# Recurrent mixer: sigmoids as tanh, roots and reciprocals as a power on GpSimd, and k and r loaded one tile ahead

## The reference, cut to what matters

```
w_log = -softplus(-(w0 + tanh(wd) @ w_up)) - 0.5
decay = exp(-exp(w_log))              # = exp(-const * sigmoid(w0 + ...))
a     = sigmoid(a0 + ad @ a_up)
kk    = head_l2norm(k * k_k)          # x * rsqrt(sum(x*x over the head) + 1e-12)
k_eff = k * (1 + (a - 1) * k_a)
...                                    # the recurrence over positions, y = its output
yn    = (y - mean) * rsqrt(var + 64e-5) * ln_g + ln_b     # per head
out   = (yn + bonus) * (sigmoid(gd) @ g_up)
```

## Time and profile before

| | |
|---|---|
| time, median of 3 | 4488.01 us (4481.62 to 4489.07) |
| profiled execution, its own time | 4496.26 us |
| its span | 4494.6 us |
| recurrent mixer phase in it | about 2068 to 2872 us |
| granted TensorE clock, mean | 0.961 of full speed |

### The profile page before, as it was taken

One profiled execution on the slowest core, in us unless ns is written; L12 is line 12 of the kernel. 1 busy time (PEld: TensorE's weight loads), 2 busy tenths in 40 slices (PEclk: granted clock), 3 DMA queues, 4 the chain that ended last, 5 costly groups with the idle time before them and its releaser, 6 DMA issues. The chain is left out here.

```text
span 4494.6 us, 74705 instructions
## 1 busy us (share of the span) xinstructions
PE 4000.6 (89%) x29550; PEld 2823.7 (63%) x29550; DVE 2819.5 (63%) x5982; ACT 1519.4 (34%) x3304; POOL 867.1 (19%) x908
## 2 busy tenths in 40 slices
PE   8989999988999899998989999898999788777776
PEld 6747887756888686786877778687444333333332
DVE  5674433775432566756666666335778888888885
ACT  3353242354433336613555554332111111111111
POOL 1101010100200101100000000000344444444443
PEclk9999999999999999998999999899999988999999
DMA  4213443301443310231000000333999999999998
GB/s 129 81 39 110 146 133 99 115 19 57 154 146 104 133 38 20 99 108 39 15 17 20 24 23 6 127 113 128 381 405 421 421 409 415 414 405 412 413 410 330
DMA packets 150605, 795.18 MB, mean 177 GB/s; under 512 B 19896, under 2 KB 23208, under 8 KB 83440
## 3 DMA queue, kind: packets, MB, share of 16 engines
q0 software_dynamic: 84496, 574.75, 31.8%
q1 hardware_dynamic: 58272, 188.32, 12.9%
q10 hardware_dynamic: 7488, 27.30, 1.8%
HBM read 766.11 MB, written 20.00 MB: 175 GB/s over the span
## 5 line engine op out<-in xcount | busy, mean ns | idle before, releaser
L3189 PE MATMUL psum<-rows,diag 128*128 128x512 f32 x2048 | 994.1, 635 | 238.2 <-ACT diag L3068 226.7
L3189 PEld LDWEIGHTS psum<-rows,diag 128*128 128x128 f32 x2048 | 405.9, 203 | 783.5 <-issue 770.5
L2930 DVE SCALAR_TENSOR_TENSOR uh<-rows,h_rows 128x1024 f32<-128x1024 f32 x512 | 627.8, 1226 | 209.8 <-DMA rows<-in_peer_uv,sel_idx 183.6
L2887 POOL DMA_INDIRECT rows<-in_peer_uv,sel_idx x512 | 606.9, 1185 | 751.9 <-PE psum L3189 697.3
L529 DVE TENSOR_TENSOR w_split_lo<-w_raw,w_split_hi 128x1024 fp32r<-128x1024 f32 (+1 forms) x271 | 326.4, 1214 | 493.9 <-ACT w_split_hi L516 489.6
L516 ACT CAST w_split_hi<-w_raw 128x1024 fp32r<-128x1024 f32 (+1 forms) x271 | 276.4, 1027 | 613.9 <-PE psum L465 395.2
L3061 ACT ACTIVATE g<-g 128x4 f32<-128x4 f32 x128 | 26.3, 205 | 1089.2 <-DVE g L2941 1089.2
L693 POOL TENSOR_TENSOR uT_lo<-normed_rows,uT_hi 128x512 fp32r<-128x512 f32 x64 | 90.1, 1408 | 663.5 <-ACT uT_hi L669 663.5
L465 PE MATMUL psum<-hT_mlp_hi,w_split_hi 128*128 128x512 f32 x512 | 201.8, 394 | 5.0 <-DVE hT_mlp_lo L261 4.9
L465 PE MATMUL psum<-hT_mlp_lo,w_split_hi 128*128 128x512 f32 x512 | 201.0, 393 | 0.0
L465 PE MATMUL psum<-hT_mlp_hi,w_split_lo 128*128 128x512 f32 x512 | 200.8, 392 | 0.0
(11 more groups left out here) (526 smaller groups left out, 8650.3 us busy)
## 6 DMA issues: line engine op xcount, KB each, us to landing
w_raw<-in_w_in SPq DMA_DIRECT2D x105, 512.0 KB
w_raw<-in_w_up SPq DMA_DIRECT2D x64, 512.0 KB
w_raw<-in_w_down SPq DMA_DIRECT2D x64, 512.0 KB
amask_sb<-in_w_mod ACTq DMA_DIRECT2D x48, 512.0 KB, 4.8
wq<-in_peer_wq SPq DMA_DIRECT2D x24, 512.0 KB
rows<-in_peer_uv,sel_idx POOLq DMA_INDIRECT x512
qkpad<-in_w_out SPq DMA_DIRECT2D x12, 512.0 KB, 5.2
w_raw<-in_w_out SPq DMA_DIRECT2D x12, 512.0 KB
```

The costliest lines, as they stand in the source:

```text
L2887: nc.gpsimd.indirect_dma_start(out=rows[:, n % RB, :], out_offset=None, in_=I["peer_uv"], in_offset=bass.IndirectOffsetOnAxis(ap=sel[:, t, ...
L2930: nc.vector.scalar_tensor_tensor(prod[:], rows[:, n % RB, 0:D], 1.0, h[:, t, :], ALU.mult, ALU.mult, accum_out=dots[:, (n // BATCH) % 2, s ...
L3189: last = nc.tensor.matmul(psum[:, 2 * (t % 2) + half, :], diag[:, n % (2 * BATCH), :], rows[:, n % RB, D + half * NB:D + (half + 1) * NB], ...
```

## The change

It does five things in the recurrent mixer, and leaves all else as it is.

1. Sigmoids as tanh: ScalarE computes tanh(x/2) from the same PSUM data; scale and bias are halved (the columns once, by one small VectorE instruction in the phase before), and the (1+t)/2 is folded into later constants for `a`, while for the decay one new VectorE instruction on 128x768 at slot 2 computes 0.5 t + 0.5.
2. Roots: the two Sqrt become Identity (a copy with bias), and a GpSimd `tensor_tensor` with `pow` and the exponent -0.5 (broadcast) computes root and reciprocal at once: 128x512 and 128x256 for the norm, 128x512 for the deviation. The reciprocals on VectorE go.
3. Slots: norm from 14, 22, 24, 25, 27, 28 to 11, 17, 19, 20, 21, 22 with `kk` still at 35; `wb` from 20 to 15; normalise, scale, add, multiply of `final` from 21, 23, 25, 27 to 30, 31, 32, 34.
4. `zk_tile` and `zr_tile` have two halves each; the load for tile `g` waits for the units of tile `g-2`.
5. `Y_cells` has three parts, and GpSimd presets unit `i+1` at the start of iteration `i`, ahead of the powers.

```diff
         @block.gpsimd
+            def presets(u):
+                if u >= 3:
+                    pool.wait_ge(n_ready, 12 * (u - 2))
+                for b in range(3):
+                    nc.gpsimd.tensor_copy(Y[:, u % 3, batch(b)], mask(cst["eye"])).then_inc(y_preset, 1)
+            def inverse_norms(g):
+                for half, (lo, hi) in enumerate((LO, HI)):
+                    pool.wait_ge(norm_copied, 2 * g + half + 1)
+                    nc.gpsimd.tensor_tensor(nrm[:, lo:hi], nrm[:, lo:hi], power(hi - lo), ALU.pow).then_inc(inverse_ready, 1)
+            def inverse_deviations(g):
+                pool.wait_ge(var_copied, g + 1)
+                nc.gpsimd.tensor_tensor(sq[:], sq[:], power(S), ALU.pow).then_inc(ln_inverse, 1)
+            presets(0)
+            inverse_norms(0)
+            for i in ITERATIONS:
+                build, scanned, prep, norm, tile, final = stages(i)
+                if prep:
+                    presets(prep)
+                if final is not None:
+                    inverse_deviations(final)
+                if norm is not None:
+                    inverse_norms(norm)
...
         @block.sync
-                    if g:
-                        sp.wait_ge(k_ready, 2 * g)
-                        sp.wait_ge(r_ready, 2 * g)
-                        sp.wait_ge(rk_ready, g)
+                    if g >= 2:
+                        sp.wait_ge(k_ready, 2 * (g - 1))
+                        sp.wait_ge(r_ready, 2 * (g - 1))
+                        sp.wait_ge(rk_ready, g - 1)
-                    sp.dma_start(zk[:], R["zk_d"][g]).then_inc(rk_loaded, 16)
-                    sp.dma_start(zr[:], R["zr_d"][g]).then_inc(rk_loaded, 16)
+                    sp.dma_start(zk[:, g % 2], R["zk_d"][g]).then_inc(rk_loaded[g % 2], 16)
+                    sp.dma_start(zr[:, g % 2], R["zr_d"][g]).then_inc(rk_loaded[g % 2], 16)
...
         ScalarE
-                nc.scalar.activation((dec, aa)[w][:, lo:hi], psum[:, 7, 0:hi - lo], ACT.Sigmoid,
-                                     bias=prm[:, g, 2 * w + d:2 * w + d + 1]).then_inc(opened, 1)
+                nc.scalar.activation((dec, aa)[w][:, lo:hi], psum[:, 7, 0:hi - lo], ACT.Tanh, scale=0.5,
+                                     bias=prm[:, g, 10 + 2 * w + d:11 + 2 * w + d]).then_inc(opened, 1)
-                elif k == 25:
+                elif k == 20:
-                    nc.scalar.activation(nrm[:, 0:512], psum[:, norm_bank(g, 0), :], ACT.Sqrt, bias=cst["tiny"][:]
-                                         ).then_inc(norm_roots, 1)
+                    nc.scalar.activation(nrm[:, 0:512], psum[:, norm_bank(g, 0), :], ACT.Identity, bias=cst["tiny"][:]).then_inc(norm_copied, 1)
...
-                    nc.scalar.activation(sq[:], psum[:, 7, :], ACT.Sqrt, bias=cst["ln_eps"][:], scale=1.0 / 64
-                                         ).then_inc(ln_root, 1)
+                    nc.scalar.activation(sq[:], psum[:, 7, :], ACT.Identity, bias=cst["ln_eps"][:], scale=1.0 / 64
+                                         ).then_inc(var_copied, 1)
...
         VectorE
+                if k == 2:
+                    dve.wait_ge(opened, 4 * u + 2)
+                    nc.vector.tensor_scalar(dec[:], dec[:], 0.5, 0.5, ALU.mult, ALU.add).then_inc(shares_ready, 1)
...
-                elif k == 20:
+                elif k == 15:
-                    nc.vector.tensor_tensor(wb[:], cells(nrm[:]), cells(Lc[:]), ALU.mult).then_inc(wb_ready, 1)
+                    nc.vector.scalar_tensor_tensor(wb[:], cells(nrm[:]), -0.5, cells(Lc[:]), ALU.mult, ALU.mult).then_inc(wb_ready, 1)
...
-                elif k in (18, 20):
-                    dve.wait_ge(ln_root, g + 1)
-                    nc.vector.reciprocal(sq[:, at], sq[:, at]).then_inc(ln_inverse, 1)
-                elif k == 21:
-                    dve.wait_ge(ln_inverse, 2 * g + 2)
+                elif k == 30:
+                    dve.wait_ge(ln_inverse, g + 1)
                     nc.vector.tensor_tensor(yb[:], yb[:], sq[:], ALU.mult).then_inc(normed, 1)
```

More of the change, by code:

```diff
@@ L1990, in rwkv_phase, with power @@
         ob_stored = (ob_stored0, ob_stored1)
+        rk_loaded = (rk_loaded0, rk_loaded1)
         @block.gpsimd
         def _(pool):
[L1994 to L1998, removed]
+            def power(n):
+                return cst["power"][:].to_broadcast([P, n])
+            def presets(u):
[20 more added lines that the diff above has]
+                    inverse_norms(norm)
         @block.sync
@@ L2159, in lora_product @@
                     elif d == 0:
[L2160 removed]
+                        pe.wait_ge(norm_copied, 2 * (g + 1))
                     elif g >= 2:
@@ L2189, in norm_product @@
             def norm_product(k, g):
-                if k == 24:
+                if k == 19:
                     pe.wait_ge(squared, g + 1)
@@ L2223, in _ @@
             lora_product(2, 0)
-            norm_product(24, 0)
-            norm_product(27, 0)
+            norm_product(19, 0)
+            norm_product(21, 0)
             lora_product(4, 0)
@@ L2319, in norm_steps @@
             def norm_steps(k, g):
-                if k == 22:
+                if k == 17:
                     act.wait_ge(kr_ready, g + 1)
@@ L2529, in finals @@
                     nc.vector.tensor_tensor(ob_tile(g), yb[:], psum[:, 7, :], ALU.mult).then_inc(ob_ready, 1)
-            norms(14, 0)
-            prepare(3, 0)
-            prepare(4, 0)
-            for k in (29, 31, 33, 35):
-                norms(k, 0)
+            norms(11, 0)
+            for k in (2, 3, 4):
+                prepare(k, 0)
+            norms(35, 0)
             for i in ITERATIONS:
@@ L2664, in rwkv_constants @@
     out["ln_eps"] = np.full((P, 1), RW_LN_EPS, f)
+    out["power"] = np.full((P, 1), -0.5, f)
     return out
@@ L3298, in second_block_program @@
         cst = {n: share.take(list(I["rwc_" + n].shape)[1:]) for n in T["rwc_names"]}
-        R = {"cst": cst, "prm": share.take([DC, 10]), "up": share.take([2, 2, P]), "gup": share.take([DC, P]),
+        R = {"cst": cst, "prm": share.take([DC, 16]), "up": share.take([2, 2, P]), "gup": share.take([DC, P]),
              "zr_d": z_d["r"], "zk_d": z_d["k"], "zv_d": z_d["v"]}
@@ L3355, in sb @@
             return rw.enter_context(nc.sbuf_tensor(name, shape, dt))
-        R["zr"] = sb("zr_tile", [P, S])
+        R["zr"] = sb("zr_tile", [P, 2, S])
+        R["zk"] = sb("zk_tile", [P, 2, N_ALL])
         R["zv"] = sb("zv_tile", [P, L_CH + N_ALL])
-        for n in ("zk", "kk", "kr", "nrm", "dec", "Lc", "eR", "aa"):
+        for n in ("kk", "kr", "nrm", "dec", "Lc", "eR", "aa"):
             R[n] = sb(n + "_tile", [P, N_ALL])
@@ L3361, in second_block_program @@
         R["AT"] = sb("AT", [P, NCH, L_CH])
-        for n in ("Y", "BT", "bt", "kt"):
+        R["Y"] = sb("Y_cells", [P, 3, NCH, L_CH])
+        for n in ("BT", "bt", "kt"):
             R[n] = sb(n + "_cells", [P, 2, NCH, L_CH])
```

83 lines of the change are left out of this document (39 added, 44 removed).

## The result

The changed kernel takes 5913.5 us (median of 4 runs, 5903.2 to 5917.2) against 4488.5 us for the kernel before (4 runs, 4481.6 to 4489.6). The ratio is 1.317 with a 95% interval of 1.314 to 1.319. The forecast was 4465 us with a range up to 4505; the time lies 1408 us above that range. The profiled execution has a span of 5901.3 us, before it was 4494.6: 1406.7 us more.

The account below looks back on a forecast made before the run. PE was taken to nearly bound the mixer, so only its idle microseconds could be won. Removed 40.4 us, added 6.0 and 11.9, gave -22.5: the median 4488.0 becomes 4465.5 us, range 4430 to 4505.

Parts of the forecast that it names:

- (h): GpSimd's power in norm and final: 8 us for 512 columns, 12 for 768, costing 11.9 us together.
- the late power: Rival, 0.22: power outlasts its window, 4505 to 4579 us; P, its 768-column time, cancels the other gains at 16 us.
- (a): Exp table loads on PE's path in iterations 1 to 14: 17.9 us gained; Sigmoid loads counted 0.
- (b): `final`, seven times in iterations 3 to 15: Sqrt load in the `W_cells` wait 9.0 us, two reciprocals 4.9, gained.
- (c): Granted clock: three iterations at 0.96 expected to recover 1.4 us each, 4.2 gained, 0 as the other end.
- (d): Norm, six times in iterations 2 to 12: one load goes, Square stands before `W_cells`; 0.3 us each, 1.8 gained.
- (e): k and r loaded a tile ahead: a tenth of VectorE's 26 us of waits before `kr`, 2.6 us gained.
- (f): New 128x768 VectorE instruction at slot 2 delays the second Gram product's masked copy: 0.4 us, 15 times, 6.0 cost.
- (g): Tail of `final` at slots 30 to 34 shares VectorE with masked copies: 0 cost, without cover about 1 us each.
- The quick power: Rival, 0.20: power takes 1.3 us for 512 columns and 2.0 for 768; 4448 us, 4430 with Sigmoid loads on the path.
- a load costs as much again in drain: Rival, 0.02: the engine drains around each table load, another 1.28 us at 21 places on the path; 4438 us.
- The refilled waits: Rival, 0.11: PE waits for the next thing instead, two thirds of the 34 us vanish, power's 12 remain; 4488 us.

Follow-up runs that it names:

- run 6: Changed kernel with the power on only the first eighth of the columns, the rest a multiplication on GpSimd (output not the reference's): 4492.2 us, ratio 1.0004.
- run 1: Changed kernel with the GpSimd power replaced by a multiplication of the same tiles and shapes (output not the reference's): 4425.1 us, ratio 0.986.
- run 11: Changed kernel with the cheap multiplication for the power and the copies out of PSUM made as Sqrt: table loads return, no reciprocals (output not the reference's); 4454.7 us.
- run 12: Changed kernel with VectorE reciprocals in place of the power, plain copies instead of Sqrt, final's last steps at slots 21 to 27 (output not the reference's): 4444.6 us.
- run 2: Kernel before with sigmoids as tanh and k and r loaded a tile ahead, its roots kept: 4466.8 us, ratio 0.994.
- run 9: Changed kernel with only the roots undone (Sqrt on ScalarE, reciprocals on VectorE, final's last steps back at slots 21 to 27): 4464.7 us, ratio 0.995.
- run 4: Kernel before with k and r loaded a tile ahead alone: 4487.0 us, ratio 0.9992.
- run 5: Changed kernel with both roots as logarithm and exponential on ScalarE, without the GpSimd power or reciprocals: 4494.7 us, ratio 1.001.
- run 8: Kernel before with scratch powers and multiplications of several forms added on GpSimd behind the mixer's last presets; run once, read by its rows, no time given.

## Why the prediction was wrong

**The step that failed is (h), the power's duration**: "I take 8 us for 512 columns and 12 for 768", with 12 us as the upper end. It takes 81.9 and 123.0, ten times as long. The 5.2 us for one costly function came from VectorE's ratio of reciprocal to copy, carried over to GpSimd. No row showed that GpSimd pays for a function at VectorE's ratio, and for this one it pays some 56 times a multiplication, not 4 or 8. So the range's upper end was no bound but a second guess of the same kind. The prediction's own sign of being wrong, VectorE waiting for GpSimd at `kk` or at slot 30, is what the trace shows. The cause of the 0.16 us per column inside the engine stays open; the runs show only on what it does not depend.

**The mechanism and its law were right, and stood in the text as the rival of the late power.** With P = 123 its terms are 116.8 in the lead-in, 78.8 at the end, 112.3 in iteration 0, 6 x 109 in the norms and 7 x (82 - 13) in the finals, 1445 us together; less the 34.4 that the rest was to give, 4488 becomes 5899. Measured: 5913. That the sum comes so near is in part luck, for two errors in it cancel. The windows, taken as 14 us in the norms and 13 in the finals, were shorter: 123.0 - 112.5 = 10.5 by the changed kernel's waits in the norm ((908.5 - 121.3) / 7 = 112.5), 10.7 by run 6, and 81.9 - 69.9 = 12.0 in the finals. With 10.5 and 12.0 the terms are 28 us larger. And the rest of the change gave some 24 us more than was priced, as is shown below. The same two errors stand behind the point of 16 us, which run 6 puts near 17.5. The shorter norm window is that of iteration 0 in every iteration.

**The other terms.** They were of the right kind, and all but (f) near the right size.

- (a) Exp loads, 17.9 us. The 14 waits stood where they were looked for, with 1.43 us each, 20.0 in all, and tanh alone took them away. The Sigmoid loads, priced at 0, show no wait of PE.
- (b) `final`, 13.9. In run 1 the wait for `W_cells` is 0.47 where it was 1.87, seven times, and six waits of 0.71 for X are gone: 14.1. Run 11 confirms the load, 1.40 each. The reciprocals seem worth less: with them a final iteration takes 44.3 us in run 12 and 43.9 in run 1.
- (c) Clock, 4.2. The three iterations at 0.96 are gone, 1.5 us each; of the iterations 0 to 14 of run 1 only iteration 0 is below 1.00 (0.96). With the loads back such iterations return, but not everywhere. Each of the six iterations 3 to 13 with a final has the wait of 1.87 us in runs 2, 9 and 11; 0.96 shows in one of them in run 2, three in run 9 and six in run 11. What decides it stays open.
- (d) Norm, 1.8. Eleven waits for `S_cells`, 7.7 us, are gone. Six waits for `W_cells` of 0.84 us behind the early Square are new, 5.0 us. That leaves 2.7.
- (e) Loads ahead, 2.6 forecast and 2.6 measured. The interval of the measurement reaches to nothing, so it confirms no size; and the gain lies in iteration 0 (run 4), not spread over the tiles.
- (f) 6.0 us of cost: not seen. PE's waits there rose by 0.6 us in all, tanh alone shortens iterations 4 and 5 by 2.6 us where their two waits at the Exp were 2.9, and without the instruction on VectorE the time is the same.
- (g) 0. No cost is seen: iterations with the final's late tail are 43.9 us, the shortest of any kernel here.

In sum the rest of the change gives 64.5 us (run 1), where the prediction had 34.4, and 40 with a power as quick as run 1's. The profiles of the two kernels show 60.7 of it in the mixer. Iterations 1 to 14 are 43.5 us shorter (654.6 and 611.2), the stretch from the first `kr` to iteration 0 is 5.1 shorter and that behind iteration 14 4.8, where the prediction had 4 and 2 for the ends. Iteration 0 is 7.3 shorter (44.0 and 36.7), and there the prediction had looked only at the power's window: 3.1 of it come with the loads ahead (run 4), and 3.2 are lost again with the reciprocals (run 12). So the missing 24 us are above all (f) and iteration 0; the rest is a microsecond or two in several terms.

**What the rivals were worth.** The quick power, 4448 and 4430 at its end, is the nearest to run 1, which at 4425 is still below it; the Sigmoid loads that were to give the lower end gave nothing. That a load costs as much again in drain is not what the rows show: in run 5, too, each function starts 0.01 us after its load. A load on the path cost 1.40 us of waiting in the finals of run 11, and 1.5 more where the clock fell. The refilled waits came in small: PE's waits for `S_cells` went from 28.7 to 1.0 us, and the new ones for `W_cells` are 5.0. The doubling rule for two-input work on GpSimd, from the GPSIMD Engine Reference (the Trainium skill, § 3.1), which would give 7.0 us for 512 columns, is refuted by the row of 81.9 for this operation. For the multiplication it comes near: 0.73 us for 128x256 in run 8, where VectorE's product of that size (L2408 of the changed kernel, one input in PSUM) takes 0.42. The contention of that page's § 1 is not what made the power long, since it takes 81.9 us while VectorE stands still. Nor do most of VectorE's instructions beside the power have two SBUF inputs, as the prediction read: from 2300.9 to `kk` in iteration 4 of the kernel before it is 3 of 18, the others are masked copies out of PSUM, transposes, reciprocals and a copy.

**The chances.** 0.22 for slower was given to overruns of 4 to 10 us. The case of an operation that no row shows needed its own tail. I wrote "No row shows one", and then let a chain of two ratios set the upper end.

## What to carry to other kernels

An operation that no trace has shown on that engine has no upper bound from its neighbours: run it once by itself, at two sizes, before a schedule is built on it. Until then give the far side a real chance, and work out, as here, the duration at which the change turns over; 16 us against a measured 123 would have decided, even with errors of several us in it. When moving work off an engine, compare the new length with the window in front of its consumer: 123 us into 10.7 can't be hidden however idle the engine is. Sort PE's waits by where they stand before pricing them: of 29 waits for `S_cells` in one row of the list 14 belonged to the Exp and 11 to the norm. And price the first iteration like the others: 7.3 us of the gain lay there.

## What the runs showed of the hardware

GpSimd's power of f32 takes 0.16 us per column, 10.5 us for 64, 41.2 for 256, 82.0 for 512, with 8, 64 or 128 partitions, exponents of -0.5 or 2, broadcast or not; a multiplication of 128x256 takes 0.73 us. A logarithm and an exponential behind it made two table loads each time in run 5, 32 in all. Where PE waits 1.87 us behind a load of 1.28 us, the granted clock of the iteration is 0.96 in six of six such iterations in run 11, in three of six in run 9 and in one of six in run 2; with 0.47 us in that place (run 1) it is 1.00 in all six. Waits of PE of 69 to 113 us go with 0.65 to 0.68 (changed kernel, iterations 2 to 13). There the same matmuls also take longer: iterations 2 and 3 together have PE busy 87.4 us (2113 matmuls) in the changed kernel and 84.7 us (2114) at a clock of 1.00 in run 1.
